# One ring of 22 slots, unrolled and in order of use, for the weights of the eight experts of a hybrid decoder step

## What is computed

```python
def swiglu(h, w1, w3, w2):
    return (jax.nn.silu(h @ w1) * (h @ w3)) @ w2

def moe_swiglu(h, router, w1, w3, w2):
    logits = (h @ router).astype(jnp.float32)
    top_v, top_i = lax.top_k(logits, TOP_K)          # TOP_K = 2 of N_EXPERTS = 8
    probs = jax.nn.softmax(top_v, axis=-1)
    gate = jnp.sum(jax.nn.one_hot(top_i, N_EXPERTS) * probs[..., None], axis=-2)
    out = jnp.zeros(h.shape, jnp.float32)
    for e in range(N_EXPERTS):
        out = out + gate[..., e:e + 1] * swiglu(h, w1[e], w3[e], w2[e])
    return out
```

## Time and profile before

| what | value |
|---|---|
| time, median of 3 runs | 2499.25 us (2497.41 to 2500.42) |
| time of the profiled execution | 2499.8 us, span 2498.0 us |
| PE busy | 2434.0 us, 97% of the span |
| PEld busy | 2026.7 us, 81% |
| DVE, ACT busy | 1287.7 us (52%), 606.7 us (24%) |
| hardware_dynamic DMA queue q1 (all tensors) | 496.44 MB, 53.6% of 16 engines' span |
| instruction queue q8 | 219 packets, 3.59 MB |
| instruction queue q14 | 53 packets, 0.43 MB |
| granted clock | 0.997 |

### The profile page before, as it was taken

How to read it: one execution, slowest core, us unless ns; L and a number is a source line. 1 busy time by engine, 2 the same in 40 slices (tenths; PEclk the granted TensorE clock), 3 DMA queues, 4 the chain that set the end, 5 groups by cost and what they waited for, 6 DMA issues and landing times. The chain is left out here.

```text
span 2498.0 us, 104094 instructions
## 1 busy us (share of the span) xinstructions
PE 2434.0 (97%) x45930; PEld 2026.7 (81%) x45930; DVE 1287.7 (52%) x3333; ACT 606.7 (24%) x1798; POOL 0.2 (0%) x4
## 2 busy tenths in 40 slices
PE   9999999999999999999999999999999999999998
PEld 8987666666698999898766666669899989888887
DVE  7666666666686675756666566668311111111111
ACT  2233333433311100223332334331111111111111
POOL 0000000000000000000000000000000000000000
PEclk9999999999999999999999999999999999999999
DMA  6334432222243453423443222223799999999997
GB/s 250 112 137 162 148 137 88 83 84 80 92 153 128 153 179 127 142 106 139 164 161 127 85 77 84 84 105 145 297 356 398 380 376 409 396 379 402 395 390 308
DMA packets 146064, 500.46 MB, mean 200 GB/s; under 512 B 18784, under 2 KB 23520, under 8 KB 143360
## 3 DMA queue, kind: packets, MB, share of 16 engines
q1 hardware_dynamic: 145792, 496.44, 53.6%
HBM read 476.08 MB, written 20.29 MB: 199 GB/s over the span
## 5 line engine op out<-in xcount | busy, mean ns | idle before, releaser
L302 PE MATMUL psum<-hT,ring 128*64 128x144 f32 (+1 forms) x4568 | 457.1, 346 | 3.4 <-DVE hT L2422 1.7
L455 PE MATMUL psum<-work,ring 128*64 128x88 f32 (+3 forms) x11264 | 417.5, 232 | 15.4 <-DMA ring<-w_ff_dram 5.7
L455 PEld LDWEIGHTS psum<-work,ring 128*64 128x64 f32 x11264 | 399.2, 136 | 34.6 <-issue 29.6
L302 PEld LDWEIGHTS psum<-hT,ring 128*64 128x64 f32 x4568 | 291.8, 137 | 97.0 <-issue 11.7
L2958 DVE TENSOR_TENSOR work<-psum,work 128x88 f32<-128x88 f32 (+3 forms) x176 | 42.4, 241 | 361.8 <-PE psum L455 361.6
L2659 PE MATMUL psum<-work,proj 128*64 128x88 f32 (+3 forms) x5632 | 204.8, 232 | 6.8 <-issue 5.6
L2659 PEld LDWEIGHTS psum<-work,proj 128*64 128x64 f32 x5632 | 197.5, 136 | 14.0 <-issue 11.5
L1768 ACT ACTIVATE work<-psum 128x256 f32<-128x256 f32 (+4 forms) x320 | 103.9, 362 | 349.9 <-PE psum L1679 84.8
L302 PE MATMUL psum<-y_ret,work 128*64 128x144 f32 x2400 | 157.8, 288 | 0.8 <-DVE y_ret L532 0.8
L302 PE MATMUL psum<-work 128*64 128x144 f32 (+4 forms) x2096 | 154.1, 282 | 4.3 <-DVE work L1259 3.6
L302 PEld LDWEIGHTS psum<-y_ret,work 128*64 128x64 f32 x2400 | 150.2, 138 | 1.3 <-issue 1.3
(11 more groups left out here) (518 smaller groups left out, 3723.9 us busy)
## 6 DMA issues: line engine op xcount, KB each, us to landing
ring<-w_ff_dram SPq DMA_DIRECT2D x424, 512.0 KB, 7.6
ring<-w_mix_dram SPq DMA_DIRECT2D x256, 512.0 KB, 4.2
proj<-w_ff_dram SPq DMA_DIRECT2D x128, 512.0 KB, 5.5
proj<-w_ff_dram SPq DMA_DIRECT2D x64, 384.0 KB, 5.7
work<-s_gla_dram SPq DMA_DIRECT2D x8, 1024.0 KB, 5.0
gla_s_out<-work SPq DMA_DIRECT2D x8, 1024.0 KB, 4.7
work<-s_ret_dram SPq DMA_DIRECT2D x8, 512.0 KB, 5.6
ret_s_out<-work SPq DMA_DIRECT2D x8, 512.0 KB, 3.0
```

The lines of the kernel that those rows point to most:

```text
L302: last = nc.tensor.matmul(out[64 * c:64 * c + 64], weights[:, 64 * c:64 * c + 64], x, start=start, stop=stop)
L455: mm = nc.tensor.matmul(out[64 * c:64 * c + 64], ring[:, s, k, 64 * c:64 * c + 64], rhs[:, k0 + k, :], start=(k0 + k == 0), stop=(k0 + k = ...
```

## The change

The two rings become one of 22 slots: 2 in `lora_w`, 2 in `hT`, 2 in `y_ret`, 6 in `proj`, the 8 of `ring`, 2 in `merged`, all idle buffers by then. Each expert has 66 full slabs (44 up, 22 down; the down weights are repacked without gaps, so that an output block is 2.75 slabs), and 66 is three times 22, so a slab has the same slot in each pass. SP loads them strictly in order of use; slab n waits for slab n - 22 to be used. Two slabs share a semaphore, so PE waits once for a pair. The first 22 are issued during the merging stage as buffers come free. On PE both inner loops (over groups of 8 up slabs, and over pairs of output blocks) are written out, since slot numbers no longer repeat with them; the loop over the passes of a class stays. The loads for a dummy expert and the wait for them at the end are gone. ACT waits for the down products on `slab_done` or on a new signal `down_ps`.

```diff
+EX_RING = 22
+EX_DOWN = D // 128 * FT // KT
+EX_SLABS = UP_SLABS + EX_DOWN
...
+    EX_AT_LORA, EX_AT_HT, EX_AT_Y, EX_AT_PROJ, EX_AT_RING, EX_AT_MERGED = 0, 2, 4, 6, 12, 20
...
@@ merging stage, SP @@
             else:
-                for j in range(RING):
-                    load_ff_slab(sp, 1, j, j, FF0 + j - RING + 1)
+                for s in range(RING):
+                    sp.wait_ge(slab_done, slabs_before(layer, S_RW_OUT) + s + 1)
+                    sp.dma_start(ring[:, s], w_mix[layer, BASE[S_RW_OUT] + RING + s]).then_inc(slab_in[s], 16)
+                    if s == 3:
+                        sp.wait_ge(slab_done, join_done(0))
+                        ahead(*range(EX_AT_LORA, EX_AT_HT))
+                sp.wait_ge(slab_done, join_done(JOIN_GATES - 1))
+                ahead(*range(EX_AT_HT, EX_AT_PROJ))
+                load_first_group(sp, S_OUT)
+                sp.wait_ge(slab_done, join_done(OUT0 - 1))
+                ahead(*range(EX_AT_PROJ, EX_AT_RING))
+                for q in range(OUT0, JOIN_PAIRS):
+                    sp.wait_ge(slab_done, join_done(q))
+                    ahead(EX_AT_RING + 2 * (q - OUT0), EX_AT_RING + 2 * (q - OUT0) + 1)
+                ahead(*range(EX_AT_MERGED, EX_RING))
@@ experts, SP @@
-            p = 0, 0
-            for d in range(DRING):
-                load_down(p, 1, d)
-            for n in range(RING, UP_SLABS):
-                load_up(p, 1, n)
-            rest = passes(sp)
-            load_following(0, expert_of(slice(0, 1)), 1)
-            for d in range(DRING, DOWN_SLABS):
-                load_down(p, 1, d)
+            def load(p, e, n):
+                sp.wait_ge(slab_done, count(p, EX_SLABS, FF0 + n - EX_RING + 1))
+                sp.dma_start(ex_slot[n % EX_RING], w_ff[e, n]).then_inc(pair_in[n % EX_RING // 2 * 2], 16)
+
+            for n in range(EX_RING, EX_SLABS):
+                load((0, 0), 1, n)
...
             with sp.Fori(0, after_first) as i:
...
+                for n in range(EX_SLABS):
+                    load((i, 1), e, n)
@@ experts, PE @@
+            def up(p, cap, n):
+
+                if n % 2 == 0:
+                    pair_here(p, n)
+                pe.wait_ge(sig("w3_free" if n % 2 else "w1_free"), count(p, FT, n // 2 + 1))
                 if n in (2, 3):
                     pe.wait_ge(sig("oT"), count(p, KT, n - 1))
-                narrow_products(pe, s, bank[n % 4][:, 0:cap], hg[:, :, 0:cap])
+                for k in range(KT):
+                    for h in range(2):
+                        last = mm(bank[n % 4][64 * h:64 * h + 64, 0:cap], ex_slot[n % EX_RING][:, k, 64 * h:64 * h + 64],
+                                  hg[:, k, 0:cap], start=(k == 0), stop=(k == KT - 1))
+                last.then_inc(slab_done, 1)
...
+            def down(p, cap, m):
+
+                pe.wait_ge(sig("oT"), count(p, KT, m + 1))
+                for f in range(FT):
+                    n, k = divmod(FT * m + f, KT)
+                    if k == 0 and n % 2 == 0:
+                        pair_here(p, UP_SLABS + n)
...
             def expert(p, cap):
 
                 pe.wait_ge(sig("hg"), count(p, 1, 1))
                 settle(pe)
-                with pe.Fori(0, UP_SLABS // RING) as g:
-                    for n in range(RING):
-                        up(p, cap, n, g)
-                for n in range(UP_SLABS // RING * RING, UP_SLABS):
-                    up(p, cap, n, 0)
+                for n in range(UP_SLABS):
+                    up(p, cap, n)
                 scatter_matrix(p)
...
-                settle(pe)
-                with pe.Fori(0, KT // 2) as t:
-                    for m in range(2):
-                        down(p, cap, t, m)
-                    for m in range(2):
-                        add_up(p, t, m)
-                    for m in range(2):
-                        to_tokens(p, t, m)
+                for m in range(0, KT, 2):
+                    down(p, cap, m)
+                    down(p, cap, m + 1)
+                    add_up(p, m)
+                    add_up(p, m + 1)
+                    to_tokens(p, m)
+                    to_tokens(p, m + 1)
```

More of the change, by code:

```diff
@@ L356, in build, with slabs_in @@
     slab_done = nc.alloc_semaphore(name="slab_done")
+    def slabs_in(buffer, n):
+        return buffer.rearrange("p a b -> p (a b)")[:, 0:n * D].rearrange("p (s k m) -> p s k m", s=n, k=KT)
+    EX_AT_LORA, EX_AT_HT, EX_AT_Y, EX_AT_PROJ, EX_AT_RING, EX_AT_MERGED = 0, 2, 4, 6, 12, 20
+    pair_in = {s: slab_in[s - EX_AT_RING] if EX_AT_RING <= s < EX_AT_MERGED else nc.alloc_semaphore(name=f"pair_in{s}")
+               for s in range(0, EX_RING, 2)}
+    ex_slot = [x[:, i] for x, n in ((slabs_in(lora_w[:, :, :], 2), 2), (slabs_in(hT[:, :, :], 2), 2),
+                                    (slabs_in(y_ret[:, :, :], 2), 2), (slabs_in(proj[:, :, :], 6), 6),
+                                    (ring, RING), (slabs_in(merged[:, :, :], 2), 2)) for i in range(n)]
     rank_in = [nc.alloc_semaphore(name=f"rank_in{s}") for s in range(2)]
@@ L2158, in _, with ahead @@
         def _(sp):
-            load_group(sp, S_RW_OUT, 1)
-            load_first_group(sp, S_OUT)
+            def ahead(*slots):
+                for n in slots:
+                    sp.dma_start(ex_slot[n], w_ff[1, n]).then_inc(pair_in[n // 2 * 2], 16)
             if dense:
+                load_group(sp, S_RW_OUT, 1)
+                load_first_group(sp, S_OUT)
                 for j in range(FF_SLABS):
@@ L2554, in _ @@
-                for d in range(DRING, DOWN_SLABS):
-                    load_down(p, e, d)
+                e = sp.value_load(ctl[0:1, bass.ds(i, 1)], min_val=0, max_val=NE)
+                for n in range(EX_SLABS):
+                    load((i, 1), e, n)
             for k in range(0, KT, 2):
@@ L2559, in _ @@
             sp.wait_ge(sig("stored"), 4 * 16)
[L2560 to L2564, removed]
         @block.tensor
@@ L2627, in gather_tokens, with pair_here @@
                     last.then_inc(sig("hg_ps"), 1)
[L2629 to L2636, removed]
+            def pair_here(p, n):
+                s = n % EX_RING
+                earlier = 0
+                if EX_AT_RING <= s < EX_AT_MERGED:
+                    earlier = fills_before(layer, s - EX_AT_RING) + fills(len(STREAM), s - EX_AT_RING)
+                pe.wait_ge(pair_in[s], count(p, EX_SLABS // EX_RING * 32, earlier * 16 + (n // EX_RING + 1) * 32))
+            def up(p, cap, n):
+                if n % 2 == 0:
+                    pair_here(p, n)
+                pe.wait_ge(sig("w3_free" if n % 2 else "w1_free"), count(p, FT, n // 2 + 1))
                 if n in (2, 3):
                     pe.wait_ge(sig("oT"), count(p, KT, n - 1))
-                narrow_products(pe, s, bank[n % 4][:, 0:cap], hg[:, :, 0:cap])
+                for k in range(KT):
[3 more added lines that the diff above has]
+                last.then_inc(slab_done, 1)
             def scatter_matrix(p):
@@ L2647, in scatter_matrix @@
                 last.then_inc(sig("scatter_ps"), 1)
[L2649 to L2661, removed]
@@ L2663, in add_up @@
-            def add_up(p, t, m):
+            def down(p, cap, m):
[4 more added lines that the diff above has]
+                        pair_here(p, UP_SLABS + n)
+                    for h in range(2):
+                        last = mm(DOWN[m % 2][64 * h:64 * h + 64, 0:cap],
+                                  ex_slot[(UP_SLABS + n) % EX_RING][:, k, 64 * h:64 * h + 64], hid[:, f, 0:cap],
+                                  start=(f == 0), stop=(f == FT - 1))
+                    if k == KT - 1:
+                        last.then_inc(slab_done, 1)
+                    elif f == FT - 1:
+                        last.then_inc(sig("down_ps"), 1)
@@ L2665, in add_up @@
+            def add_up(p, m):
                 if m == 0:
                     pe.wait_ge(sig("hg"), count(p, 1, 2))
-                pe.wait_ge(sig("otok"), t * 2 + count(p, KT, m + 1))
-                pe.wait_ge(sig("added"), t * 2 + count(p, KT, m + 1))
+                pe.wait_ge(sig("otok"), count(p, KT, m + 1))
+                pe.wait_ge(sig("added"), count(p, KT, m + 1))
                 for h in range(2):
-                    last = mm(ADD[m][64 * h:64 * h + 64, 0:T], otok[0:CAP, m, 64 * h:64 * h + 64], scatter[0:CAP, :], start=True,
-                              stop=True)
+                    last = mm(ADD[m % 2][64 * h:64 * h + 64, 0:T], otok[0:CAP, m % 2, 64 * h:64 * h + 64], scatter[0:CAP, :],
+                              start=True, stop=True)
@@ L2672, in add_up, with to_tokens @@
                 last.then_inc(sig("sc_ps"), 1)
-            def to_tokens(p, t, m):
-                pe.wait_ge(sig("oT"), t * 2 + count(p, KT, m + 3))
-                nc.tensor.transpose(OTOK[m][0:CAP, 0:128], oT[:, m, :], ident).then_inc(sig("otok_ps"), 1)
+            def to_tokens(p, m):
+                pe.wait_ge(sig("oT"), count(p, KT, m + 3))
```

(14 more changed lines are left out.)

15 lines of the change are left out of this document (1 added, 14 removed).

## The result

The changed kernel takes 2603.47 us (median of 4 runs, 2598.06 to 2606.82) against 2499.32 us before (4 runs beside it): a ratio of 1.0415, 95% interval 1.040 to 1.043. It is slower by 104 us. The profiled execution took 2606.8 us, its span is 2605.0.

What follows compares the result with a forecast made beforehand. It took PE to outrun the expert weight DMAs at fewer columns; written-out code raised the passes from 711.7 to 728 + 14 = 742 us, so 2499.8 became 2530 us. Range 2477 to 2568, the forecast's own 2506 to 2555.

Steps and rivals of the forecast that it cites:

- Perfect delivery: Eight expert passes with all weights in time: 671.4 us against 711.7 now.
- the ring's own worth: Expert passes: 22 slots by themselves save 35 us, with about 4 us of waiting left in the last pass.
- Number of packets: Instruction queue q8: some 342 packets against 219 before, 18 in each written-out pass.
- What a packet costs: Code packet in saturated expert passes: between 4.0 and 6.2 us; 4.9 us taken for the up part.
- balance: Up part: PE settles at DMA's pace, 3.8 slabs or 4.9 us a packet, so 56.3 us in each pass.
- dearer packets: Rival: the wait stays long even with few loads queued; 5.3 us a packet gives 2565 us; chance 0.10.
- The two stalls: PE idle 1.39 us in the fifth pass, 1.89 in the seventh; each packet usable 6.2 us after the preceding entry.
- The jump back: Start of each class's second pass, four times: code fetched on demand, 3.5 us each (2.5 to 6.2), 14 us in all.
- the clock: PE in the expert passes: clock granted in full, 1.00 in every pass; no cost was set for it.
- Hidden code: Rival: code requests come in time with one load in flight, nothing is lost, 2465 us; chance 0.12.
- hidden crossings with jumps paid: Rival: next packet comes before PE needs it, the head of the loop does not; 2479 us; chance 0.07.
- the body stays: Rival: 18 packets are kept, so second passes run free; 704 us for the passes, 2492 in all; chance 0.08.

Runs made afterwards that it cites:

- run 4: Kernel before with each expert weight load cut to a quarter (128 KB), the rest of the weights left out: 2450.3 us.
- run 3: Changed kernel with each expert weight load cut to a quarter (128 KB), the rest of the weights left out: 2469.5 us.
- run 6: Changed kernel with expert weight loads of 256 KB (2 KB packets), half of the expert weights left out: 2484.2 us.
- run 9: Kernel before without dummy loads, with ten up slabs instead of eight, up loop of four turns and four slabs after it: 2494.26 us, ratio 0.9976.
- run 8: Kernel before without dummy loads, with fourteen up slabs instead of eight, up loop of three turns and two slabs after it: 2502.87 us, ratio 1.0017.
- run 5: Changed kernel with each slab load issued as two DMAs of 64 partitions (256 KB each), same bytes: 2945.2 us.

## Why the prediction was off

The direction came as forecast and by the mechanism named. The time, 2603.5, lies 73 us above the forecast of 2530 and above the range. Taken by its steps:

- **Perfect delivery: nearly right; the ring's own worth: open.** 671.4 us were worked out; run 4 gives 662.4, so the matmul rates taken were a little slow (32.4 ns at 72 columns; in run 4's last pass 176 matmuls take 5.72 us, 31.4 ns each from start to start). That 22 slots are worth 35 us is shown by no run, since none has them without the written-out code; fourteen slots in a loop gave no gain, ten some 4 us.
- **Number of packets: right.** 342 forecast, 346 came; 18 or 19 a pass; no DMA in the chain; merging stage within 1.4 us; landing times of the expert loads no longer than before (medians 4.6 to 6.2 us, before 5.5 to 8.4).
- **What a packet costs: this is the step that failed.** The text took 4.9 us by a balance: "The stable point in the up part is PE at DMA's pace." Its premise, a wait that depends on the loads queued, is right (the table above). The balance is not. It had the queue empty as soon as PE is slower than DMA. But at most entries (55 of 87) 16 to 24 packets, two to three loads, are outstanding, at a DMA share of 0.88 to 0.95. With 122 matmuls of 33 ns PE frees nearly four slabs in 4 us, and a load of 512 KB takes 3.9 us (median) from issue to landing even in the dense feed-forward part of run 3, so two of them are still under way when the next packet is entered. That last sentence is argued from rows; no run took it apart. Measured is the price: of the 59 packets with a stall at both ends the middle half took 5.5 to 6.3 us, a wait of some 3.1 to 3.9 us and 2.4 us to use. Over all 144 crossings, stalled or not, it is (820.6 - 24)/144 = 5.5 us in the forecast's own sum. It lay in the text as a rival, dearer packets (at 5.3 us, 2565), and even that was too low. The two stalls read as an upper end, 6.2 us a packet, were close to the common case.
- **What this makes in the sum.** The forecast's crossings cost 728 - 671.4 = 57 us of idle time. The trace has 124.1 us of "issue"; less some 24 for the jumps that is 100, so 43 us missed.
- **The jump back: right in kind, too cheap.** 5.31, 5.73, 5.54 and 5.63 us instead of 3.5, and 0.42 and 1.64 us behind two of them: 24 instead of 14 us. With light traffic it is 3.3 to 4.0 (run 3), so latency is most of it.
- **A term that was not there: the clock.** The earlier trace rows had it at 1.00 throughout, and the forecast kept it there. Its windows around the last jump (columns as in the windows above):

```profile
2487.00:2492.50 5.50, 0.00 (x0) 0.00 (x0) 0.10 (x1) 1.60 (x3) 0.00 (x0) 0.83 0.50 180
2492.50:2498.40 5.90, 4.18 (x66) 3.98 (x68) 0.00 (x0) 0.23 (x1) 0.00 (x0) 0.50 0.12 40
2498.40:2501.50 3.10, 3.10 (x66) 3.10 (x64) 0.23 (x1) 0.23 (x1) 0.00 (x0) 0.60 0.73 267
2501.50:2510.50 9.00, 8.62 (x271) 8.43 (x267) 2.31 (x7) 0.93 (x4) 0.00 (x0) 1.00 0.90 317
```

After 5.6 us of standing still the clock granted is 0.50, the 1.2 GHz level, and 53 matmuls take 3.40 us (64 ns each) where 64 take 2.17 (34 ns) six us later. Summed over the eight windows, (1 - clock) x time is 23 us. Part of the low clock falls on idle time: PE is busy for 34.9 us of it, so the loss is at most half of that, 17 us.
- **The sum closes, but not on the forecast's base.** 671.4 + 124.1 + 23 = 818.5 comes near the 820.6 measured by luck: the first term is 9 us too long, the third at least 6. By the runs it is 662.4 (run 4) + 124.1 of idle time + at most 17 of clock, and 17 us are left. An estimate accounts for them: a matmul record is 0.23 us long (L2630, median 230 ns) while the next begins 0.03 us later, so at each stall 0.2 us of the last one stand alone and are counted as busy, 93 x 0.2 = 19 us. A stall thus costs 0.2 us more than its idle time says. The sum is then at most 822.
- **Rivals.** Hidden code (2465) and hidden crossings with jumps paid (2479) are what runs 3 and 6 come near to, with less to move; at full traffic both fall. That the body stays fell with the stalls at all four jumps; 5.9 packets stay (run 9), 6.3 not always (run 8). The balance was also what kept up parts at 56.3 us; they take 61 to 67, that of the seventh pass 63.8, from 2385.6 to 2449.4 us.

The rule that the prediction quoted from the Trainium skill ("Runtime: NRT & Kernel Launch", Instruction fetch mechanics), crossings mostly hidden and a forced fetch after a far jump, agrees with run 3 in both parts, and with the changed kernel in the second alone. The figure of 128 KB from the Trainium skill ("Advanced Engine Details and Errata", ISA Cache) would be 8 packets; run 8 shows a refetch at 6.3 already, at one of four jumps.

The Trainium skill ("DMA: Bandwidth & Descriptors", Arbitration) says that a DMA engine goes round its queues and drains one packet of typically 9 to 17 descriptors, at most 64, before it changes. No row here shows such a group. By the page's figures the limit of about 22 transfers ahead of a code packet would be one to two and a half of them, an estimate; the growth with what is outstanding below 22 would fit an engine that drains what it already has. Why the limit lies there stays open.

## What to carry to other kernels

Before writing out a loop in a stretch where weights come at the full rate of DMA, count the packets of code (here 245 PE instructions each) and price each at all the weight packets that may stand before it (22 x 0.16 us) plus 2.4 us, not at an average; if the engine works through a packet in less, that difference is lost each time. A deeper ring is worth having only as far as the code that repeats stays small enough to be kept: ten slots in a loop gave 0.24%, twenty-two slots written out cost 4%. And a stall has a second price when the clock falls behind it.

## What the runs showed of the hardware beyond that

- A load of 64 partitions instead of 128 moves its 4 KB packets in 276 ns (median) instead of 159, 238 GB/s in all at a full DMA share (run 5).
- A code packet for an idle queue starts 1.05 to 1.16 us after the preceding one is entered and is usable 2.2 to 2.6 us later, so the floor of a packet is some 3.5 us: PE at 72 columns (4.0 us a packet) is just above it.
- What is kept does not end at the code of one inner loop: a whole pass of 5.9 packets with two loops in it is at hand for the next pass (221 q8 packets in run 9, 219 before), 6.3 is not always (232, refetched at one of four jumps), 12 and 18 are not.
